# Scatter turns between the pieces of the last pair's down projection

## The chip, the cores and the metric

The kernel runs on one core of a Trainium2 chip. The metric is the device time of one execution in microseconds, as a median of several runs. The engines' short names are those of the profile: PE is TensorE (PEld its weight loads, PEldq its sequencer), DVE is VectorE, ACT is ScalarE, POOL is GpSimd, SP is SyncE, which here issues DMA transfers.

## The reference

A two-layer encoder on 256 tokens of width 2048, in float32. Each layer adds a mixer (latent attention, dilated attention and an mLSTM side by side) to `x`, and then a mixture of 16 experts, of which each token takes two:

```
for l in range(DEPTH):
    xn = rms_norm(x, norm_mix[l])
    ...
    x = x + jnp.concatenate([y_mla, y_dil, y_ml], axis=-1) @ w_out[l]
    x = x + hier_moe(rms_norm(x, norm_ffn[l]), ...)

def hier_moe(x, wg, bg, we, be, w_gate, w_up, w_down):
    ...                       # comb: weight of each expert for each token, zero but for two
    h = jax.nn.silu(jnp.einsum('bsd,edf->bsef', x, w_gate)) * jnp.einsum('bsd,edf->bsef', x, w_up)
    h = h * comb[..., None].astype(h.dtype)
    return jnp.einsum('bsef,efd->bsd', h, w_down)
```

An expert has 512 hidden units, so `w_down` is 512 by 2048 for each. The change is in the end of this part.

## The kernel before

**Experts in pairs.** The 16 experts go in eight pairs `i` = 0 to 7. For each expert up to 64 tokens (`CAP`) are gathered by a matmul with a one-hot matrix; the two experts of a pair stand side by side as 128 rows. PE then multiplies by the gate and up weights in two halves each (`expert("g0")`, `"u0"`, `"g1"`, `"u1"`), turns the product (`turn_h`), multiplies by the down weights and adds the rows back to their tokens.

**Down projection.** The down weights of an expert come in two blocks (`dn0`, `dn1`), 1024 output columns each, 16 KB a partition, laid out as four runs `k` of 1024 columns (128 hidden units each). Each block makes two tiles of 512 columns in PSUM: `dy0`, `dy1` from the first, `dy2`, `dy3` from the second, in banks 4 to 7. The two experts' matmuls use 64 columns of the array each and run side by side; a float32 matmul shows as two MATMUL records. ACT copies `dy0` and `dy2` to `Y` in SBUF (line 2509), DVE `dy1` and `dy3` (line 2191).

**Scatter.** Eight turns `sc0` to `sc7`: turn `k` multiplies columns 256k to 256k+255 of `Y` by the weighted one-hot matrix `Sw` (two matmuls, four records), and DVE adds the result to `X` (`add_moe`, line 2131). Pair `i - 1` is scattered during pair `i`. The last pair, 7, is scattered after its own down projection, in order, in banks 1, 2, 3, 0, 1, 2, 3, 0.

**The last pair** is handled apart (lines 1368 to 1383). Its weights come in halves of a block: `load_halves` (line 727) issues for each block the first half of both experts and then the second, and PE waits for the second halves in the middle of a block. A half is `k` = 0, 1 for all 1024 columns. So the loop runs `k` outside and the two tiles inside, and `dy2` and `dy3` are done together at the end:

```
for k in range(4):
    if k == 2:
        for j in range(2):
            pe.wait_ge(*loaded(f"dn{half}{j}_{i}", l))
    for q, name in enumerate(names):
        for j in range(2):
            ...
```

**Between the down projection and the last turns** stands a branch (line 1393; on DVE line 2194): if an expert had more than 64 tokens, a loop over all experts (the sweep) would compute the rest. The inputs here never take it. The two layers are written out one behind the other, so each has its own branch.

**Behind the turns.** In layer 0 DVE and ACT scale each finished pair of `X` tiles into `XN` for the next layer (`gained`; even tiles DVE, line 1522, odd tiles ACT, line 2241); PE's next matmuls, the projection `c0`, take the tiles in order, then two more projections and a matmul on the sum of squares. SP lets the next layer's loads go once `sc0` is made. In layer 1 SP sends each finished pair of `X` tiles to the output (line 774). A slot of weights may be overwritten once its last reader is done (`LAST_READER`).

All PE matmuls here are recorded by one helper, line 833; DVE's adds have line 2131.

Of the kernel before, what the change touches and what calls it, by code (L numbers as in the profile page):

```python
# [26 lines left out]
P = 128  # L27
# [172 lines left out]
def plan_banks():  # L200
# [61 lines left out]
    for i in range(NE // 2):  # L262
        b.once(f"g0_{i}", 0)
        b.once(f"u0_{i}", 1)
        b.once(f"g1_{i}", 2)
        b.once(f"ht0_{i}", 0)
        if i + 1 < NE // 2:
            for n in range(4):
                b.once(f"gx{n}_{i + 1}", 4 + n)
        b.once(f"u1_{i}", 3)  # L270
        for k in range(KT // 2):
            if k == KT // 4:
                b.once(f"ht1_{i}", 3)
            if i >= 1:
                b.once(f"sc{k}_{i - 1}", SCATTER_BANKS[k])
        b.once(f"sw_{i}", 0)
        for n in range(4):
            b.once(f"dy{n}_{i}", 4 + n)
    for k in range(KT // 2):
        b.once(f"sc{k}_{NE // 2 - 1}", LAST_BANKS[k])  # L280
    return b
# [93 lines left out]
LAST_READER.update({f"m{j}": f"{('c21', 'c12')[j % 2]}_{j // 2}" for j in range(2 * N_PAIR)})  # L375
LAST_READER.update({f"{n}{j}_{i}": f"{n}_{i}" for n in ("g0", "u0", "g1", "u1") for j in range(2) for i in range(NE // 2)})
LAST_READER.update({f"dn{half}{j}_{i}": f"dy{2 * half + 1}_{i}" for half in range(2) for j in range(2) for i in range(NE // 2)})

# [15 lines left out]
def build(nc, a, consts, onehot, lncount, out):  # L396
    with ExitStack() as ctx:
# [3 lines left out]
        def sem(name):  # L401
            return ctx.enter_context(nc.semaphore(name))
# [130 lines left out]
        dve_steps, act_steps = sem("dve_steps"), sem("act_steps")  # L533
        par_in, small_in = sem("par_in"), sem("small_in")
        pieces_in = {name: sem(f"pieces_in_{name}") for name in IN_PIECES}
        halves_in = {f"{n}{j}": sem(f"halves_in_{n}{j}") for n in ("g0", "u0", "g1", "u1", "dn0", "dn1") for j in range(2)}
        x_out, x_back = sem("x_out"), sem("x_back")
        x_in, c0_in = [sem(f"x_in{q}") for q in range(4)], [sem(f"c0_in{q}") for q in range(3)]
# [28 lines left out]
        def bank(name):  # L567
            return ps[:, BANKS.where(name), :]
# [96 lines left out]
        def _(sp):  # L665
# [14 lines left out]
            for l in range(DEPTH):  # L680
# [45 lines left out]

                def load_halves(n, w):

                    for half in range(2):
                        for j in range(2):  # L730
                            name = f"{n}{j}_{NE // 2 - 1}"
                            if half == 0:
                                sp.wait_ge(*empty(name, l))
                            part = slice(half * (SLOT // 2), (half + 1) * (SLOT // 2))
                            sp.dma_start(slot(name)[:, part], w[j][:, part]).then_inc(
                                halves_in[f"{n}{j}"] if half == 0 else slot_full[SLOTS.where(name)], 16)

                for i in range(NE // 2 - 1):
                    for half in range(2):
# [91 lines left out]
        def _(pe):  # L831
# [206 lines left out]
            for l in range(DEPTH):  # L1038
# [287 lines left out]
                for i in range(NE // 2):  # L1326
                    if i == NE // 2 - 1:
                        wait_alone(pe, *after("flags", l))
                        runs, due = sweep_due(pe)
                    if i:  # L1330
                        expert("g0", i)
                        expert("u0", i)
                    expert("g1", i)
                    turn_h(0, i)
                    if i == NE // 2 - 1:
                        written(i - 1)
                        scatter(i - 1, range(KT // 4))
                    elif i:
                        gather(i + 1)
                    expert("u1", i)  # L1340
                    if i == 0:
                        gather(1, (0,))
                        turn_h(1, 0)
                        gather(1, (1,))
                    elif i == NE // 2 - 1:
                        scatter(i - 1, (4, 5))
                        turn_h(1, i)
                        scatter(i - 1, (6, 7))
                    else:
                        written(i - 1)  # L1350
                        scatter(i - 1, range(KT // 4))
                        turn_h(1, i)
                        scatter(i - 1, range(KT // 4, KT // 2))

                    pe.wait_ge(*freed(f"sw_{i}", l))
                    pe.wait_ge(*after("gw", l, i))
                    for t in range(NT):
                        last = pe.transpose(bank(f"sw_{i}")[0:2 * CAP, t * P:(t + 1) * P], Gw[:, t, :], ident)  # L1358
                    last.then_inc(*made(f"sw_{i}"))

                    for half in range(2):
                        pe.wait_ge(*copied(f"ht{half}_{i}", l))
                    for half in range(2):
                        if half and i == 0:
                            gather(1, (2, 3))
                        w = [slot(f"dn{half}{j}_{i}").rearrange("p (k c) -> p k c", k=4) for j in range(2)]
                        for j in range(2):
                            block_in(f"dn{half}{j}_{i}")
                        if i == NE // 2 - 1:
                            names = [f"dy{2 * half + q}_{i}" for q in range(2)]  # L1370
                            for name in names:
                                pe.wait_ge(*freed(name, l))
                            for k in range(4):
                                if k == 2:
                                    for j in range(2):
                                        pe.wait_ge(*loaded(f"dn{half}{j}_{i}", l))
                                for q, name in enumerate(names):
                                    for j in range(2):
                                        own_rows = slice(j * CAP, (j + 1) * CAP)
                                        last = mm(bank(name)[own_rows, :], hs[:, k, own_rows], w[j][:, k, q * 512:(q + 1) * 512], k == 0, k == 3)  # L1380
                                    if k == 3:
                                        last.then_inc(*made(name))
                            continue
                        for q in range(2):
                            name = f"dy{2 * half + q}_{i}"
                            pe.wait_ge(*freed(name, l))
                            for k in range(4):
                                for j in range(2):
                                    own_rows = slice(j * CAP, (j + 1) * CAP)
                                    last = mm(bank(name)[own_rows, :], hs[:, k, own_rows], w[j][:, k, q * 512:(q + 1) * 512], k == 0, k == 3)  # L1390
                            last.then_inc(*made(name))

                with pe.If(due > 0):

                    i = NE // 2 - 1
                    for name in [f"sc{k}_{i - 1}" for k in range(KT // 2)] + [f"sw_{i}"] + [f"dy{n}_{i}" for n in range(4)]:
                        pe.wait_ge(*copied(name, l))
                    pe.wait_ge(sweep_dve, runs * SWEEP_DVE + 1)
                    for t in range(NT):
# [14 lines left out]
                    with pe.Fori(0, NE) as e:  # L1414
# [8 lines left out]

                        pe.wait_ge(sweep_dve, runs * SWEEP_DVE + 5 + e * 2)
                        for half in range(2):
                            w = ring[:, 4 + half, :].rearrange("p (k c) -> p k c", k=4)
                            for q in range(KT // 2):
                                o = ps[:, (4 + q // 2) if half == 0 else q // 2, q % 2 * S:(q % 2 + 1) * S]
                                for k in range(4):
                                    last = mm(o, w[:, k, q * P:(q + 1) * P], hT[:, k, :], k == 0, k == 3)  # L1430
                            last.then_inc(sweep_pe, 1)
                    wait_alone(pe, sweep_dve, runs * SWEEP_DVE + SWEEP_DVE)

                pe.wait_ge(*copied(f"sw_{NE // 2 - 1}", l))
                for n in range(4):
                    pe.wait_ge(*copied(f"dy{n}_{NE // 2 - 1}", l))
                    scatter(NE // 2 - 1, (2 * n, 2 * n + 1))


        def pcol(l, r):  # L1440
# [44 lines left out]
        def _(dve):  # L1485
# [120 lines left out]
            for l in range(DEPTH):  # L1606
# [555 lines left out]
                for i in range(NE // 2):  # L2162
# [23 lines left out]
                        add_moe(i - 1, range(KT // 4, KT // 2))  # L2186
                    dve.wait_ge(*ready(f"sw_{i}", l))
                    dve.tensor_copy(Sw, bank(f"sw_{i}")[0:2 * CAP, 0:S]).then_inc(*read(f"sw_{i}"))
                    for n in (1, 3):
                        dve.wait_ge(*ready(f"dy{n}_{i}", l))  # L2190
                        dve.tensor_copy(Y[:, n * 512:(n + 1) * 512], bank(f"dy{n}_{i}")[0:2 * CAP, :]).then_inc(*read(f"dy{n}_{i}"))  # L2191

                runs, due = sweep_due(dve)
                with dve.If(due > 0):
# [28 lines left out]
                        ins.then_inc(sweep_dve, 1)  # L2223
                    wait_alone(dve, sweep_dve, runs * SWEEP_DVE + SWEEP_DVE)
                for k in range(KT // 2):
                    add_moe(NE // 2 - 1, (k,))
                    if l + 1 < DEPTH:
                        dve.wait_ge(*copied(f"sc{k}_{NE // 2 - 1}", l))
                        gained(2 * k, l + 1)
# [309 lines left out]
def laid_out(inputs):  # L2539
# [13 lines left out]
    def columns(*rows):  # L2553
# [9 lines left out]
            "w_main": tiled(w_in[:, :, D_DQ:C_IN - 4 * H_M], CH), "w_up": up, "w_mqk": mqk,  # L2563
            "w_out_a": w["w_out"][:, :K_A * P].reshape(DEPTH, K_A, P, N_OUT, CH)[:, list(A_ROWS)].transpose(0, 3, 2, 1, 4).reshape(DEPTH, N_OUT, P, 2 * HALF_A), "w_out_b": w["w_out"][:, K_A * P:].reshape(DEPTH, K_B, P, N_BPAIR, 2, CH).transpose(0, 3, 2, 4, 1, 5).reshape(DEPTH, N_BPAIR, P, 4 * HALF_B), "w_router": tiled(router, P // GROUPS)[:, 0], "params": params, "params96": params96, "biases": biases, "x_t": x_t,
            "moe_w_gate": tiled(w["moe_w_gate"], CH), "moe_w_up": tiled(w["moe_w_up"], CH),
            "moe_w_down": tiled(w["moe_w_down"], 4 * CH)}


# [15 lines left out]
```

## Time and profile before

| | |
|---|---|
| median of 3 runs | 1823.3 us (1821.94, 1823.3, 1828.55) |
| span of the profiled execution | 1824.6 us |
| granted PE clock, mean | 0.997 |
| PE busy | 1816.0 us (100%), 12238 matmul records |
| DVE, ACT busy | 737.0 us (40%), 314.4 us (17%) |
| DMA | 546.92 MB, mean 300 GB/s |

The profiled execution is told by its span, first to last instruction; the page has no other time for it. Layer 0 ends and layer 1 begins near 917 us. A row of a timeline gives the start, the duration, the engine, the line, the operation, output and inputs, and how many alike were merged; in brackets the idle time ahead and what ended it. Matmuls overlap in their pipeline, so the time between two starts is what one costs, not its duration.

### The profile page before, as it was taken

The numbers are of one execution on the slowest core, as the hardware profiler recorded it, in microseconds if no ns is written. First come the engines' busy times: TensorE is split into PE (matmuls) and PEld (weight loads), VectorE is DVE, ScalarE is ACT, GpSimd is POOL, SyncE is SP. The second block draws the span as 40 slices with busy tenths as digits, with TensorE's granted clock in tenths as the row PEclk, the third lists the DMA queues.
The fourth block names the chain that finished last, engine by engine and source line by source line (L and its number), as shares of the span: only waits on it lengthen the run. The fifth ranks groups of instructions, "written<-read, shape, count | busy, mean of one in ns | idle before, by whom it ended". The sixth has DMA issues, their size and how long they took to land.

```text
span 1824.6 us, 28274 instructions
## 1 busy us (share of the span) xinstructions
PE 1816.0 (100%) x12238; PEld 1377.6 (76%) x12238; DVE 737.0 (40%) x1531; ACT 314.4 (17%) x846; POOL 13.9 (1%) x27
## 2 busy tenths in 40 slices
PE   9999999999999999999999999999999999999999
PEld 9788887899765667656597888878996666676665
DVE  3477665676202121121235675656761021221213
ACT  3123122212101111011021231222121011110110
POOL 1000000000000000000000000000000000000000
PEclk9999999999999999999999999999999999999999
DMA  9433343447899999999884342444579999999997
GB/s 385 165 139 142 147 168 141 189 163 287 341 425 424 426 428 426 427 427 421 346 356 150 133 178 112 167 177 153 200 283 358 421 425 427 426 428 427 426 422 305
DMA packets 51439, 546.92 MB, mean 300 GB/s; under 512 B 5872, under 2 KB 6000, under 8 KB 14576
## 3 DMA queue, kind: packets, MB, share of 16 engines
q1 hardware_dynamic: 48816, 531.47, 71.1%
q0 software_dynamic: 2496, 13.57, 2.0%
q8 instruction: 102, 1.67, 0.4%
q14 instruction: 25, 0.20, 0.0%
HBM read 540.78 MB, written 4.24 MB: 299 GB/s over the span
## 4 chain that ended last, share of the span: by engine, by line
PE 99%; DMA 0%; issue 0%; DVE 0%; SPq 0%; DVEq 0%
PE ps L833 96%; PE ps L887 1%; PE ps L1191 1%; PE ps L1299 1%; PE ps L903 0%; PE ps L895 0%; DMA ring<-in_w_lat 0%; PE ps L1358 0%; PE ps L986 0%; DVE ring L1892 0%; PE ps L1072 0%; PE ps L1099 0%; PE ps L1138 0%; DVE X L1921 0%; DVE X L2131 0%
## 5 line engine op out<-in xcount | busy, mean ns | idle before, releaser
L833 PE MATMUL ps<-ring,scr 128*64 128x256 f32 (+2 forms) x3488 | 624.6, 423 | 0.1
L833 PEld LDWEIGHTS ps<-ring,scr 128*64 128x64 f32 (+1 forms) x3488 | 336.9, 138 | 212.7 <-issue 119.3
L833 PE MATMUL ps<-ring,XN 128*128 128x256 f32 (+2 forms) x1184 | 242.2, 361 | 1.2 <-DMA ring<-in_w_lat 1.2
L833 PEld LDWEIGHTS ps<-ring,XN 128*128 128x128 f32 x1184 | 210.7, 190 | 21.7 <-issue 2.3
L833 PE MATMUL ps<-ring,X 128*128 128x256 f32 x896 | 200.6, 379 | 0.0
L833 PE MATMUL ps<-XN,ring 128*128 128x128 f32 (+1 forms) x1312 | 195.8, 306 | 0.0
L833 PEld LDWEIGHTS ps<-XN,ring 128*128 128x128 f32 x1312 | 180.2, 191 | 12.7 <-issue 3.1
L833 PEld LDWEIGHTS ps<-ring,X 128*128 128x128 f32 x896 | 169.6, 190 | 22.7
L833 PE MATMUL ps<-PR,scr 128*64 128x256 f32 (+2 forms) x704 | 173.8, 402 | 0.0
L2167 DVE TENSOR_TENSOR v_mla<-scr,ps 128x256 f32<-128x256 f32 x32 | 13.5, 421 | 390.6 <-PE ps L833 390.6
L833 PE MATMUL ps<-BIAS,scr 128*64 128x256 f32 (+1 forms) x608 | 157.2, 414 | 0.0
L833 PE MATMUL ps<-XN,scr 128*64 128x256 f32 (+1 forms) x480 | 141.3, 451 | 0.0
L833 PEld LDWEIGHTS ps<-v_mla,PR 128*128 128x128 f32 x1024 | 117.3, 193 | 4.2 <-issue 4.2
L833 PE MATMUL ps<-v_mla,PR 128*128 128x128 f32 x1024 | 120.2, 277 | 0.0
L833 PE MATMUL ps<-PR,prob 128*128 128x256 f32 x512 | 117.7, 382 | 2.3 <-issue 2.3
L833 PEld LDWEIGHTS ps<-PR,scr 128*64 128x64 f32 (+1 forms) x704 | 98.0, 144 | 25.6 <-issue 3.4
L833 PEld LDWEIGHTS ps<-PR,prob 128*128 128x128 f32 x512 | 94.6, 190 | 21.3 <-issue 9.8
L2191 DVE COPY prob<-ps 128x512 f32<-128x512 f32 x32 | 22.1, 692 | 207.4 <-PE ps L833 207.4
L833 PEld LDWEIGHTS ps<-BIAS,scr 128*64 128x64 f32 x608 | 81.8, 137 | 29.5 <-issue 2.9
L2494 ACT ACTIVATE scr<-ps,par 128x128 f32<-128x128 f32 x240 | 64.7, 407 | 220.1 <-PE ps L833 220.1
L2131 DVE TENSOR_TENSOR X<-X,ps 128x512 f32<-128x512 f32 x128 | 87.9, 688 | 28.0 <-PE ps L833 27.1
L833 PEld LDWEIGHTS ps<-XN,scr 128*64 128x64 f32 x480 | 65.3, 137 | 34.2 <-issue 25.0
(276 smaller groups left out, 1454.7 us busy)
## 6 DMA issues: line engine op xcount, KB each, us to landing
ring<-in_moe_w_gate SPq DMA_DIRECT2D x38, 2048.0 KB, 20.2
ring<-in_w_main SPq DMA_DIRECT2D x36, 2048.0 KB, 9.5
ring<-in_moe_w_down SPq DMA_DIRECT2D x32, 2048.0 KB, 22.2
ring<-in_moe_w_up SPq DMA_DIRECT2D x30, 2048.0 KB, 17.3
ring<-in_w_out_a SPq DMA_DIRECT2D x16, 1280.0 KB, 6.0
PR<-in_moe_w_up SPq DMA_DIRECT2D x10, 2048.0 KB, 16.3
XN<-in_moe_w_down SPq DMA_DIRECT2D x10, 2048.0 KB, 19.2
ring<-in_moe_w_up SPq DMA_DIRECT2D x20, 1024.0 KB, 21.5
```

The lines of the kernel that those rows point to most:

```text
L833: return pe.matmul(o, lhsT, rhs, start=start, stop=stop, skip_group_check=True)
L887: last = pe.transpose(bank(name)[:, (kt * NT + t) * P:(kt * NT + t + 1) * P], prob[:, u % 2, j, t, kt * P:(kt + 1) * P], ident)
L1191: last = pe.transpose(bank(f"xt{j}")[:, q * P:(q + 1) * P], X[:, 4 * g + q, t * P:(t + 1) * P], ident)
L1299: last = pe.transpose(bank(name)[:, q * 2 * CAP:(q + 1) * 2 * CAP], gated[:, (2 * half + q) * P:(2 * half + q + 1) * P], ident)
L2131: dve.tensor_tensor(x, x, bank(name), ALU.add).then_inc(*read(name))
L2167: dve.tensor_tensor(gated[:, half * CH:(half + 1) * CH], sgs[:, half * CH:(half + 1) * CH], bank(f"u{half}_{i}")[0:2 * CAP, 0:CH], ALU.mul ...
L2191: dve.tensor_copy(Y[:, n * 512:(n + 1) * 512], bank(f"dy{n}_{i}")[0:2 * CAP, :]).then_inc(*read(f"dy{n}_{i}"))
L2494: ins = act.activation(XG[:, 4 * n + k, :], bank(name)[:, k * 2 * CAP:(k + 1) * 2 * CAP], ACT.Copy, scale=pcol(l, R_FFN + 4 * n + k))
```

## The change

The down weights are laid out anew, in all eight pairs: a block is four runs `n` of 256 output columns, and each holds its four `k`. A matmul of 512 columns reads two runs of 256, which lie 1024 elements apart. The last pair now finishes a piece of columns before it begins the next: `dy0`, `dy1`, `dy2` with 512 columns, and `dy3`, `dy4` with 256 each (`dy4` in bank 4, which `dy0` had). Its second block is loaded in three pieces for each expert (a half and two quarters). The turns 0 and 1 stand between `dy1` and `dy2`, 2 and 3 between `dy2` and `dy3`, 4 and 5 between `dy3` and `dy4`, and 6 and 7 stay behind the branch. DVE's adds follow, so that in layer 0 the `gained` steps of the first six turns come behind DVE's branch, without the adds. The sweep reads its weights in the new layout and waits for more banks. Lines that follow from this alone are left out:

```diff
+    b.once(f"dy4_{NE // 2 - 1}", 4)
...
+LAST_READER.update({f"dn1{j}_{NE // 2 - 1}": f"dy4_{NE // 2 - 1}" for j in range(2)})
...
-                    for half in range(2):
+                    for lo, hi in ((0, 2), (2, 4)) if n != "dn1" else ((0, 2), (2, 3), (3, 4)):
...
+                    def down(name, half, lo, hi):
+
+                        w = [slot(f"dn{half}{j}_{i}").rearrange("p (n k c) -> p n k c", n=4, k=4) for j in range(2)]
+                        pe.wait_ge(*freed(name, l))
+                        for k in range(4):
+                            for j in range(2):
+                                own_rows = slice(j * CAP, (j + 1) * CAP)
+                                last = mm(bank(name)[own_rows, 0:(hi - lo) * CH], hs[:, k, own_rows], w[j][:, lo:hi, k, :], k == 0, k == 3)
+                        last.then_inc(*made(name))
...
+                    if i == NE // 2 - 1:
+                        for j in range(2):
+                            block_in(f"dn0{j}_{i}")
+                        down(f"dy0_{i}", 0, 0, 2)
+                        last_blocks(0)
+                        down(f"dy1_{i}", 0, 2, 4)
+                        pe.wait_ge(*copied(f"sw_{i}", l))
+                        pe.wait_ge(*copied(f"dy0_{i}", l))
+                        scatter(i, (0, 1))
+                        for j in range(2):
+                            block_in(f"dn1{j}_{i}")
+                        down(f"dy2_{i}", 1, 0, 2)
+                        pe.wait_ge(*copied(f"dy1_{i}", l))
+                        scatter(i, (2, 3))
+                        for j in range(2):
+                            pe.wait_ge(third_in[j], 16 * (l + 1))
+                        down(f"dy3_{i}", 1, 2, 3)
+                        pe.wait_ge(*copied(f"dy2_{i}", l))
+                        scatter(i, (4, 5))
+                        last_blocks(1)
+                        down(f"dy4_{i}", 1, 3, 4)
+                        break
...
-                pe.wait_ge(*copied(f"sw_{NE // 2 - 1}", l))
-                for n in range(4):
+                for n in (3, 4):
                     pe.wait_ge(*copied(f"dy{n}_{NE // 2 - 1}", l))
-                    scatter(NE // 2 - 1, (2 * n, 2 * n + 1))
+                    scatter(NE // 2 - 1, (n + 3,))
...
+                    last = i == NE // 2 - 1
+                    for n, lo, w in ((1, 512, 512), (3, 1536, CH), (4, 1536 + CH, CH)) if last else ((1, 512, 512), (3, 1536, 512)):
                         dve.wait_ge(*ready(f"dy{n}_{i}", l))
...
+                        if last and n != 4:
+                            add_moe(i, {1: (0, 1, 2, 3), 3: (4, 5)}[n])
...
                 for k in range(KT // 2):
-                    add_moe(NE // 2 - 1, (k,))
+                    if k >= 6:
+                        add_moe(NE // 2 - 1, (k,))
                     if l + 1 < DEPTH:
...
-            "moe_w_down": tiled(w["moe_w_down"], 4 * CH)}
+            "moe_w_down": tiled(w["moe_w_down"], CH).reshape(DEPTH, NE, 2, 4, P, 4 * CH).swapaxes(3, 4).reshape(DEPTH, NE, 2, P, SLOT)}
```

## Rows read from the trace of the kernel before

**Rows 1.** The page's head and its first part.
```profile
span 1824.6 us, 28274 instructions
...
PE 1816.0 (100%) x12238; PEld 1377.6 (76%) x12238; DVE 737.0 (40%) x1531; ACT 314.4 (17%) x846; POOL 13.9 (1%) x27
```

**Rows 2.** Waits of PE, whole span: us in total, times, longest.
```profile
PE ps L833 <- issue: 2.3, 2, 1.8
PE ps L833 <- DMA ring<-in_w_lat: 1.2, 1, 1.2
PE ps L833 <- DVE eps L1494: 1.1, 1, 1.1
PE ps L833 <- DVE ring L1892: 0.3, 2, 0.2
```

**Rows 3.** PE timeline, layer 0's end: start us, us, what, [idle before].
```profile
893.00 0.64 PE L833 MATMUL ps<-ring,scr 128*64 128x512 f32 x1
...
899.92 7.32 PE L833 MATMUL ps<-ring,scr 128*64 128x512 f32 x32
...
909.05 2.40 PE L833 MATMUL ps<-PR,prob 128*128 128x256 f32 x10 [1.82 <-issue]
...
911.96 5.02 PE L833 MATMUL ps<-PR,prob 128*128 128x256 f32 x22 [0.51 <-issue]
...
916.82 18.36 PE L833 MATMUL ps<-ring,XN 128*128 128x192 f32 x114
```

**Rows 4.** PE timeline, layer 1's end.
```profile
1800.27 0.64 PE L833 MATMUL ps<-ring,scr 128*64 128x512 f32 x1
...
1807.18 7.16 PE L833 MATMUL ps<-ring,scr 128*64 128x512 f32 x32
...
1814.28 7.17 PE L833 MATMUL ps<-PR,prob 128*128 128x256 f32 x32
```

**Rows 5.** PE timeline, two changes of tile shape in the last pair.
```profile
1787.73 1.46 PE L833 MATMUL ps<-PR,prob 128*128 128x256 f32 x6
...
1789.12 0.43 PE L833 MATMUL ps<-BIAS,scr 128*64 128x256 f32 x1
...
1789.38 0.38 PE L833 MATMUL ps<-BIAS,scr 128*64 128x256 f32 x1
...
1795.86 0.38 PE L833 MATMUL ps<-BIAS,scr 128*64 128x256 f32 x1
...
1796.17 1.99 PE L833 MATMUL ps<-PR,prob 128*128 128x256 f32 x8
...
1798.01 0.38 PE L1299 MATMUL ps<-K,v_mla 128*128 128x128 f32 x2
```

**Rows 6.** Lines 1393 (branch) and 1376 (wait): ns min/median/max, first and last start.
```profile
L1393 PEldq COMPARE_BRANCH  x2: 3308/4204/5100, 903.8 to 1810.8; - x2
...
L1376 PEldq EVENT_SEMAPHORE  x4: 51/51/51, 893.7 to 1810.6; - x4
```

**Rows 7.** DVE timeline, layer 1's end.
```profile
1800.76 0.42 DVE L2188 COPY PR<-ps 128x256 f32<-128x256 f32 x1
...
1814.38 0.69 DVE L2191 COPY prob<-ps 128x512 f32<-128x512 f32 x1 [6.29 <-PE ps L833]
...
1815.87 1.99 DVE L2131 TENSOR_TENSOR X<-X,ps 128x512 f32<-128x512 f32 x3 [0.80 <-PE ps L833]
...
1821.49 0.69 DVE L2131 TENSOR_TENSOR X<-X,ps 128x512 f32<-128x512 f32 x1 [0.18 <-PE ps L833]
```

**Rows 8.** DVE and PE timelines, where the next layer begins.
```profile
918.34 0.35 DVE L1522 TENSOR_SCALAR XN<-X,par 128x256 f32<-128x256 f32 x1
...
926.01 0.43 DVE L1620 TENSOR_TENSOR scr<-PR 128x256 f32<-128x256 f32 x1
...
937.19 0.59 PE L833 MATMUL ps<-scr,ones 128*128 128x256 f32 x2
```

**Rows 9.** SP's DMA issues, second down block of layer 1.
```profile
1775.60 11.12 SPq L735 DMA_DIRECT2D ring<-in_moe_w_down  x4
```

More of the change, by code:

```diff
@@ L535, in build @@
         pieces_in = {name: sem(f"pieces_in_{name}") for name in IN_PIECES}
+        third_in = [sem(f"third_in{j}") for j in range(2)]
         halves_in = {f"{n}{j}": sem(f"halves_in_{n}{j}") for n in ("g0", "u0", "g1", "u1", "dn0", "dn1") for j in range(2)}
@@ L727, in load_halves @@
                 def load_halves(n, w):
-                    for half in range(2):
+                    for lo, hi in ((0, 2), (2, 4)) if n != "dn1" else ((0, 2), (2, 3), (3, 4)):
                         for j in range(2):
                             name = f"{n}{j}_{NE // 2 - 1}"
-                            if half == 0:
+                            if lo == 0:
                                 sp.wait_ge(*empty(name, l))
-                            part = slice(half * (SLOT // 2), (half + 1) * (SLOT // 2))
+                            part = slice(lo * (SLOT // 4), hi * (SLOT // 4))
                             sp.dma_start(slot(name)[:, part], w[j][:, part]).then_inc(
-                                halves_in[f"{n}{j}"] if half == 0 else slot_full[SLOTS.where(name)], 16)
+                                halves_in[f"{n}{j}"] if lo == 0 else slot_full[SLOTS.where(name)] if hi == 4 else third_in[j], 16)
                 for i in range(NE // 2 - 1):
@@ L1362, in _, with last_blocks @@
                         pe.wait_ge(*copied(f"ht{half}_{i}", l))
+                    def down(name, half, lo, hi):
[6 more added lines that the diff above has]
+                        last.then_inc(*made(name))
+                    def last_blocks(half):
+                        for j in range(2):
+                            pe.wait_ge(*loaded(f"dn{half}{j}_{i}", l))
+                    if i == NE // 2 - 1:
[12 more added lines that the diff above has]
+                        scatter(i, (2, 3))
+                        for j in range(2):
+                            pe.wait_ge(third_in[j], 16 * (l + 1))
[5 more added lines that the diff above has]
+                        break
                     for half in range(2):
@@ L1365, in _ @@
                             gather(1, (2, 3))
-                        w = [slot(f"dn{half}{j}_{i}").rearrange("p (k c) -> p k c", k=4) for j in range(2)]
                         for j in range(2):
                             block_in(f"dn{half}{j}_{i}")
[L1369 to L1383, printed above, removed]
-                        for q in range(2):
[L1385 to L1391, printed above, removed]
+                        for q in range(2):
+                            down(f"dy{2 * half + q}_{i}", half, 2 * q, 2 * q + 2)
                 with pe.If(due > 0):
                     i = NE // 2 - 1
-                    for name in [f"sc{k}_{i - 1}" for k in range(KT // 2)] + [f"sw_{i}"] + [f"dy{n}_{i}" for n in range(4)]:
+                    for name in [f"sc{k}_{i - 1}" for k in range(KT // 2)] + [f"sw_{i}"] + [f"dy{n}_{i}" for n in range(5)] + [f"sc{k}_{i}" for k in range(6)]:
                         pe.wait_ge(*copied(name, l))
@@ L1425, in _ @@
                         for half in range(2):
-                            w = ring[:, 4 + half, :].rearrange("p (k c) -> p k c", k=4)
+                            w = ring[:, 4 + half, :].rearrange("p (n k c) -> p n k c", n=4, k=4)
                             for q in range(KT // 2):
@@ L1429, in _ @@
                                 for k in range(4):
-                                    last = mm(o, w[:, k, q * P:(q + 1) * P], hT[:, k, :], k == 0, k == 3)
+                                    last = mm(o, w[:, q // 2, k, q % 2 * P:(q % 2 + 1) * P], hT[:, k, :], k == 0, k == 3)
                             last.then_inc(sweep_pe, 1)
                     wait_alone(pe, sweep_dve, runs * SWEEP_DVE + SWEEP_DVE)
-                pe.wait_ge(*copied(f"sw_{NE // 2 - 1}", l))
-                for n in range(4):
+                for n in (3, 4):
                     pe.wait_ge(*copied(f"dy{n}_{NE // 2 - 1}", l))
-                    scatter(NE // 2 - 1, (2 * n, 2 * n + 1))
+                    scatter(NE // 2 - 1, (n + 3,))
         def pcol(l, r):
@@ L2188, in _ @@
                     dve.tensor_copy(Sw, bank(f"sw_{i}")[0:2 * CAP, 0:S]).then_inc(*read(f"sw_{i}"))
-                    for n in (1, 3):
+                    last = i == NE // 2 - 1
+                    for n, lo, w in ((1, 512, 512), (3, 1536, CH), (4, 1536 + CH, CH)) if last else ((1, 512, 512), (3, 1536, 512)):
                         dve.wait_ge(*ready(f"dy{n}_{i}", l))
-                        dve.tensor_copy(Y[:, n * 512:(n + 1) * 512], bank(f"dy{n}_{i}")[0:2 * CAP, :]).then_inc(*read(f"dy{n}_{i}"))
+                        dve.tensor_copy(Y[:, lo:lo + w], bank(f"dy{n}_{i}")[0:2 * CAP, 0:w]).then_inc(*read(f"dy{n}_{i}"))
+                        if last and n != 4:
+                            add_moe(i, {1: (0, 1, 2, 3), 3: (4, 5)}[n])
                 runs, due = sweep_due(dve)
```

## The prediction

> **What bounds the kernel now.** I read the page's head, then what TensorE (PE) waits for, then its timeline at the end of each of the two layers, where the change lies. The head shows PE busy for 1816.0 of 1824.6 us [rows 1]. All that its matmuls wait for is a few us; the largest is 2.3 us in two waits that no data releases ("issue") [rows 2]. So the kernel is a queue of matmuls, and an edit pays only if it takes matmul time or an idle stretch of PE away. Near the change there is one such stretch. In layer 0 the second half of the down projection starts at 899.92 and the first scatter matmul at 909.05, 9.13 us later; eight turns then take until 916.82, with a 0.51 us hole [rows 3]. In layer 1 the same second half needs 1814.28 - 1807.18 = 7.10 us, with no hole behind it [rows 4]. Layer 0 thus loses 9.13 - 7.10 = 2.03 us ahead of the turns, and within them 7.77 us less 6.91 and 0.1 for the change of shape: some 0.75. The 6.91 are 32 matmuls a step of 0.216 us apart (layer 1's 32 take 7.17; less the last one's own 0.38 and that 0.1, over 31 steps). Together 2.8 us, all that can be won there; layer 1 has nothing to win.
>
> **Matmul work.** Per layer the last pair's down projection stays 13.8 us (1800.27 to 1814.1) [rows 4] and the turns 6.9 us. The eight matmuls with 512 columns that made half of the old second block become sixteen with 256 (32 more weight loads and matmuls in the stream). Two 256-column steps take 2 x 0.216 us [rows 5], one of 512 takes 6.91/16 = 0.43 [rows 4]: nothing added.
>
> **Two runs in the moving operand.** In all eight pairs the weights now lie by blocks of 256 columns, so a 512-column matmul reads two runs of 256. No row of before has that. Lower bound: 0. Upper bound from the nearest rows: each run charged like a matmul of its own, 2 x 0.216 - 0.43, some 0.003 us, for 496 such steps (248 per layer: 7 pairs x 32, and 24): 1.4 us. I take 0, since the steps of one run show no cost per run.
>
> **Switching between the two kinds of matmul.** Down steps use 64-column tiles in pairs, scatter turns full 128-column tiles. Into full tiles: 1795.86 to 1796.17 is 0.31 instead of 0.216, and eight matmuls from 1796.17 end at 1798.01 instead of 1797.90; 0.20 together. Back: 1787.73 plus six steps is 1789.03, the next starts at 1789.12, and the one after 0.26 later instead of 0.216; 0.13 together [rows 5]. Before there was one switch, down to scatter. Now there are three round trips more per layer: 3 x 0.33 = 1.0 us each, 2.0 us in all. Lower bound 0, if the queue covers them; I take 2.0, since each switch shown paid.
>
> **The branch.** Behind the down projection stands a branch over a loop that is skipped. PE's sequencer takes 5.10 us over it in layer 0 (from 903.8, so until 908.9; the scatter starts at 909.05) and 3.31 us in layer 1 (from 1810.8, until 1814.1; scatter at 1814.28) [rows 3, 4, 6]. This is the stall of layer 0, and layer 1 just escapes: the sequencer stood 3.3 us ahead of the array. It stood there because the wait ahead of the last 32 instructions was passed at 1810.6, as the array began them (1807.18 + 3.44), the branch was reached 0.2 us later, and those instructions last 3.4 us [rows 4, 6]. After the change the last 32 instructions, dy4's, are 256 wide and last 8 x 0.216 = 1.73, with the switch 1.86. The same distances give a lead of 1.86 - 0.2 = 1.66 us and a stall of 3.31 - 1.66 = 1.6 us in each layer. Bounds: 0 (the half before passed its wait at 893.7, 2.8 us before the array came to it [rows 3, 6]; such a lead covers all), and 5.10 - 1.66 = 3.4. I take 1.6, from the wait that stands where the new one will stand. The hole of 0.75 inside layer 0's turns came right behind the branch and has no data releaser; I let it go with the stretch of code that is moved.
> The page Runtime: NRT & Kernel Launch of the Trainium skill, section Instruction fetch mechanics, says that instructions are prefetched in sequence alone and that a taken branch to a target outside the window stalls until the page is fetched. By it both layers would stall, whatever the lead; the trace agrees in layer 0 (2.03 us) and not in layer 1 (none). The sum by it would lie between the forecast's and the +6.0 of the second rival. TensorE: Matmul & The Clock Gate (its table) gives PE a queue of 64. By it the sequencer would be 64 instructions ahead, which now reaches back over dy4 (32) and the turns before it, and the branch would be hidden; the wait at 1810.6, with no lead, does not agree. The sum by it would be the first rival's.
>
> **Waits of the new order.** Turn pairs (0,1), (2,3), (4,5) each wait for a copy of the block before last: dy0's copy has dy1's 3.4 us, dy1's has turns 0 and 1 and dy2, dy2's has turns 2 and 3 and dy3 (1.9 + 1.7) against 0.69 us for a copy [rows 7]. Behind each stands all of PE, so an uncovered copy would cost up to 0.8 us. dy3's copy has turns 4 and 5 and dy4. Only dy4's is close: VectorE starts such a copy 0.1 us after PE's next matmul (1814.38 against 1814.28 [rows 4, 7]), a 256-wide one takes 0.42, and turn 6 covers it with 0.87 us; without that cover 0.2. In VectorE's queue the adds of turns 0 to 5 now stand between the copies; two adds of 0.69 fit into each 1.7 us of down work.
>
> **Behind the last turn** nothing changes in layer 1: the last add starts at 1821.49 and the span ends 3.1 us later [rows 1, 7]; the earlier output transfers only leave sooner. In layer 0 VectorE and ScalarE also scale X into XN. VectorE now does six such steps (0.35 each) in a row behind its own branch, then adds 6 and 7. From the start of dy4's copy: 1.5 us to the first step (1814.38 to 1815.87 [rows 7]), 2.2 for six, 2.0 for the rest, so 5.7. The next layer's first projection starts at 1.6 + 1.9 - 0.1 = 3.4 by the same clock and asks for a pair of XN tiles every 1.29 us (0.161 us a matmul, eight a pair [rows 3]): first at 3.4 (there at 1.9), last at 12.4. The sum of squares, ready at 926.4, is used at 937.19 [rows 8]. All hidden; were there no branch stall, the first tile would be 0.4 us late.
>
> **DMA.** The second block comes in six transfers, not four. The old four were issued from 1775.60 to 1786.7 [rows 9], for a block used at 1807.18 [rows 4]: 20 us of cover, so two more issues cost nothing (at most their own 0.9 us with the cover gone). The next layer's loads, let go by turn 0, leave some 7 us sooner, the third of them (it waits for dy4) 2 us later; PE had no DMA wait there to lose or gain [rows 2].
>
> **Sum** on the profiled execution (1824.6 us; the page has its span and no time around it): layer 0: 2.0/2 + 1.6 - 2.8 = -0.2; layer 1: 1.0 + 1.6 = +2.6. Together +2.4, 1827.0. The median of the three runs is 1823.3, 1.3 below the span, which gives 1825.7.
>
> **Rivals.**
> *The branch is hidden* (sequencer far enough ahead). Layer 0: 1.0 + 0.4 - 2.8 = -1.4; layer 1: 1.0 + 0.2. Sum -0.2: 1823.1; with the switches covered too, -2.2: 1821.1. For it: the lead of 2.8 at 893.7. Against it: the wait at 1810.6.
> *The branch takes 5.1 us in both layers.* 1.0 + 3.4 - 2.8 and 1.0 + 3.4: +6.0, 1829.3; in layer 0 alone +4.2, 1827.5. For it: code moves, and one of two branches took that long. Against: the other did not.
> *Slower outright: the second run of a 512-column operand costs a restart.* A first step behind a switch is 0.04 to 0.05 longer [rows 5]; with that on each of 496 steps, 23 us: 1849. It decides the sign from (9.1 - 2.4)/496 = 0.014 us a step. Against: nothing in rows of one run hints at it.
> Faster by over 0.5% has no mechanism: PE's waits come to 4.9 us in all, the start of the kernel among them [rows 2].
>
> **How the numbers follow.** Forecast 0.60, long branch in one layer or both 0.15, branch hidden 0.20, restart per run 0.04, something else faster 0.01. A measurement of this kernel can tell about 0.5%, 9.1 us, from no change; all but the last two lie within. The range reaches from the hidden branch with covered switches, 1821, to the long branch with 1.4 us for the two runs, 1830.7, and I let the spread of the runs (1821.94 to 1828.55) take the low end to 1820.5. Faster 0.01, same 0.95, slower 0.04.
>
> **What will show it.** The branch rows: each over 3 us, and a PE hole of 1 to 2 us ahead of turn 6 in both layers, none of 0.75 behind it in layer 0. Starts 0.3 us apart at each of the six switches. Steps of 512 columns still 0.43 apart in pairs 0 to 6. No PE wait for a copy or a DMA between dy0 and dy4. The forecast is wrong if layer 1's end grows by less than 1 us or more than 4, or if the time changes outside the two layer ends.

## The result and the profile after

The changed kernel took 1830.71 us (median of 5 runs, 1829.05 to 1835.14), the kernel before 1822.99 beside it: a ratio of 1.0031, 95% interval 1.002 to 1.0043; the two medians alone lie 7.7 us apart, 1.0042, at the upper end of that interval. On a second occasion it was 1.0022 (1.0011 to 1.0032). So by the ratios it is slower by 0.2 to 0.3%, 4 to 6 us, within the 0.5% that counted as no change; the forecast was +2.4 us. The profiled span went from 1824.6 to 1829.1 us.

The page's head, TensorE's waits over the whole span, and its branch, in the changed kernel (answering [rows 1, 2, 6]; line 836 is the matmul helper, line 1411 the branch):

```profile
span 1829.1 us, 28344 instructions
...
PE 1817.1 (99%) x12270; PEld 1378.0 (75%) x12270; DVE 737.2 (40%) x1533; ACT 313.8 (17%) x846; POOL 13.8 (1%) x27
...
PE ps L836 <- issue: 4.3, 2, 2.2
PE ps L836 <- DMA ring<-in_w_lat: 2.7, 1, 2.7
...
L1411 PEldq COMPARE_BRANCH  x2: 3882/3910/3938, 912.3 to 1819.9; - x2
```

PE's timeline at the end of layer 0, after (answering [rows 3]): the five pieces of down work, the turns two by two between them, and the next layer's first matmul.

```profile
894.01 0.64 PE L836 MATMUL ps<-ring,scr 128*64 128x512 f32 x1
...
901.03 1.99 PE L836 MATMUL ps<-PR,prob 128*128 128x256 f32 x8
902.95 3.65 PE L836 MATMUL ps<-ring,scr 128*64 128x512 f32 x16
906.54 1.99 PE L836 MATMUL ps<-PR,prob 128*128 128x256 f32 x8
908.46 1.95 PE L836 MATMUL ps<-ring,scr 128*64 128x256 f32 x16
910.34 1.99 PE L836 MATMUL ps<-PR,prob 128*128 128x256 f32 x8
912.26 1.95 PE L836 MATMUL ps<-ring,scr 128*64 128x256 f32 x16
916.34 1.96 PE L836 MATMUL ps<-PR,prob 128*128 128x256 f32 x8 [2.13 <-issue]
918.14 17.11 PE L836 MATMUL ps<-ring,XN 128*128 128x192 f32 x106
```

The same at the end of layer 1 (answering [rows 4]), and VectorE's last add there [rows 7]:

```profile
1801.60 0.64 PE L836 MATMUL ps<-ring,scr 128*64 128x512 f32 x1
...
1817.92 1.99 PE L836 MATMUL ps<-PR,prob 128*128 128x256 f32 x8
1819.85 1.95 PE L836 MATMUL ps<-ring,scr 128*64 128x256 f32 x16
1823.98 1.96 PE L836 MATMUL ps<-PR,prob 128*128 128x256 f32 x8 [2.18 <-issue]
...
1825.98 0.69 DVE L2148 TENSOR_TENSOR X<-X,ps 128x512 f32<-128x512 f32 x1 [0.18 <-PE ps L836]
```

Where the 4.5 us of span came from, stretch by stretch: up to dy0 of layer 0 it is 894.01 against 893.00, +1.0 (below). Layer 0's end, dy0 to the next layer's first matmul: 24.13 against 23.82, +0.3. The whole middle, 918.14 to 1801.60: 883.46 against 883.45, nothing. Layer 1's end, dy0 to the last add: 24.38 against 21.22, +3.2. In both layers the time is in one hole ahead of turn 6, and the six switches.

The +1.0 was not forecast. The first weights are waited for 2.7 us instead of 1.2, and the first projection starts 0.8 us later; and right behind that wait the granted clock is 0.5 (the 1.2 GHz level, half of the other) for 3.4 us, so that this projection takes 1.6 us longer. Against that, a stretch at the low level near 455 us, which every profile here has, lasts 3.4 us where it lasted 6.8 before, some 1.7 us less lost. That makes 0.7; 0.3 us is left open. The first two rows are the first projection before and after. The third is a row by stretch: its bounds and length, the busy time of PE, PEld, DVE, ACT and POOL, the granted clock, and the DMA's share and rate.

```profile
6.95 20.61 PE L833 MATMUL ps<-ring,XN 128*128 128x192 f32 x128 [1.22 <-DMA ring<-in_w_lat]
7.72 22.21 PE L836 MATMUL ps<-ring,XN 128*128 128x192 f32 x128 [2.69 <-DMA ring<-in_w_lat]
...
7.60:10.90 3.30, 3.18 (x10) 3.21 (x11) 0.62 (x2) 0.97 (x3) 0.00 (x0) 0.50 1.03 409
```

The table gives these two ends for all kernels run (start to start, from the timelines), and PE's branch. The expectations below count layer 1 only to its last matmul, 0.4 to 0.7 us sooner than the last add.

| kernel | layer 0 end, us | layer 1 end, us | branch, us (layer 0, 1) | ratio (95%) |
|---|---|---|---|---|
| before | 23.82 | 21.22 | 5.10, 3.31 | |
| before_again | 24.89 | 21.46 | 4.72, 3.57 | 1.0003 (0.9992 to 1.0014) |
| after | 24.13 | 24.38 | 3.88, 3.94 | 1.0031 (1.002 to 1.0043) |
| after_again | 23.68 | 25.46 | 3.44, 3.93 | 1.0022 (1.0011 to 1.0032) |
| before_no_branch | 20.90 | 21.10 | none | 0.9991 (0.9979 to 1.0002) |
| after_no_branch | 22.92 | 22.40 | none | 1.0002 (0.9992 to 1.0012) |
| after_short_skip | 23.01 | 22.39 | 0.25, 0.36 | 1.0006 (0.9996 to 1.0016) |
| layout_only | 22.98 | 21.88 | 3.84, 3.56 | 0.9997 (0.9986 to 1.0007) |
| turns_behind | 25.43 | 23.81 | 5.01, 3.48 | 1.0025 (1.0016 to 1.0034) |
| two_pieces | 26.12 | 22.17 | 6.27, 3.80 | 1.0017 (1.0008 to 1.0026) |
| after_else | 28.08 | 22.40 | 7.19, 3.61 (the jump) | 1.0029 (1.0018 to 1.0041) |
| before_else | 25.81 | 21.16 | 5.78, 4.35 (the jump) | 1.0039 (1.0025 to 1.0054) |

### The profile page after: what moved, and what is told of

It reads as the page before. It is cut to its first block, busy times and chain, and to the rows that moved or that the text cites. A ratio compares the mean times of both kernels' runs of the same rounds, so it can differ in the third digit from the quotient of the medians.

```text
span 1829.1 us, 28344 instructions
## 1 busy us (share of the span) xinstructions
PE 1817.1 (99%) x12270; PEld 1378.0 (75%) x12270; DVE 737.2 (40%) x1533; ACT 313.8 (17%) x846; POOL 13.8 (1%) x27
## 4 chain that ended last, share of the span: by engine, by line
PE 99%; DMA 0%; issue 0%; DVE 0%; SPq 0%; DVEq 0%
PE ps L836 96%; PE ps L890 1%; PE ps L1194 1%; PE ps L1302 1%; PE ps L906 0%; DMA ring<-in_w_lat 0%; PE ps L898 0%; PE ps L1361 0%; PE ps L989 0%; DVE ring L1909 0%; PE ps L1102 0%; PE ps L1075 0%; PE ps L1141 0%; DVE X L1938 0%; DVE X L2148 0%
## 5 line engine op out<-in xcount | busy, mean ns | idle before, releaser
L2209 DVE COPY prob<-ps 128x512 f32<-128x512 f32 (+1 forms) x34 | 22.4, 660 | 199.4 <-PE ps L836 199.4
```

The costliest lines, as they stand in the source:

```text
L2209: dve.tensor_copy(Y[:, lo:lo + w], bank(f"dy{n}_{i}")[0:2 * CAP, 0:w]).then_inc(*read(f"dy{n}_{i}"))
```

## The experiments

**The kernel before, once more** (no edit).

> The kernel before, unchanged, profiled a second time. Theory A (the 2.8 us that layer 0 loses at its branch belong to the way the code lies): the hole is there again, second down half to first scatter matmul 9.1 us in layer 0 and 7.1 in layer 1, branch rows 5.1 and 3.3 us, span within 1 us of 1824.6. Theory B (they are an accident of the one profiled execution, which would explain why the medians differ by 7.7 us and the two profiled spans by 4.5): layer 0 shows 7.1 to 7.5 us as layer 1 does, both branches near 3.3 us, span 1820.5 to 1822.5. Time: ratio 1.000 by both.

Theory A held: the hole at layer 0's branch came again, with a second hole behind it. In its PE timeline the branch (4.72 us) leaves 1.44 and 1.06 us; a third hole is new, PE waiting 0.96 us for the second half of the second down block. In layer 1 a branch of 3.57 us, longer than the 3.31 of the first profile, leaves a hole of 0.16.

```profile
903.76 3.65 PE L833 MATMUL ps<-ring,scr 128*64 128x512 f32 x16 [0.96 <-DMA ring<-in_moe_w_down]
908.86 2.40 PE L833 MATMUL ps<-PR,prob 128*128 128x256 f32 x10 [1.44 <-issue]
912.32 5.01 PE L833 MATMUL ps<-PR,prob 128*128 128x256 f32 x22 [1.06 <-issue]
```

**The branch taken out of the changed kernel, and of the kernel before.**

```diff
-                with pe.If(due > 0):
+                if False:
```

> The changed kernel without the sweep loop and its branch on PE (the part that computes tokens beyond 64 of an expert is left out). Theory A (the hole of 2.1 us ahead of turn 6 in each layer is the branch): both holes go, dy4 to turn 6 is 0.3 us; the layer ends shorten by 2 x 2.1, less up to 0.4 each for the copy of dy4, now uncovered: 3.4 to 4.3 us off the span, some 1825. Ratio to before 1.001. Rival C (PE waits there for VectorE's copies of dy3 and dy4): the holes stay and so does the span, 1829. Ratio 1.003.

> The kernel before without the sweep loop and its branch on PE (the part that computes tokens beyond 64 of an expert is left out). Theory A: layer 0's loss of 2.8 us goes, layer 1 stays: span 1821.8 if the profiled execution of before is typical. Theory B: nothing to gain beyond what the repeated profile of before shows. In both, the changed kernel without branch stays behind this one by its six switches more per layer, 2 x 1.0 us, and up to 0.8 for the copies of dy4: 2.0 to 2.8 us. Ratio 0.9985 (A) or 1.000 (B).

Theory A held in both for the layer ends. In the changed kernel without the branch, dy4 is followed by turn 6 without a hole in either layer (1817.23 plus eight steps of 0.216 is 1818.96; the turn starts 0.15 later, the switch), so no copy was waited for, and rival C is out. What PE now waits for in layer 0 is VectorE's first XN tile.

```profile
1817.23 1.95 PE L836 MATMUL ps<-ring,scr 128*64 128x256 f32 x16
1819.11 1.99 PE L836 MATMUL ps<-PR,prob 128*128 128x256 f32 x8
...
916.46 8.85 PE L836 MATMUL ps<-ring,XN 128*128 128x192 f32 x53 [0.79 <-DVE XN L1539]
```

Without branches the changed kernel stays 2.0 us behind in layer 0 (0.8 of it that wait) and 1.3 in layer 1: the switches, some 1.2 to 1.3 us a layer. In time it is 1.0002 against 0.9991, some 2 us. The profiled span of the kernel before without the branch, 1824.0, is above A's 1821.8: 1.4 us of that lies between the layer ends, where the granted clock is 0.5 from 1358.9 to 1365.8, 6.8 us instead of the 3.4 before.

**The new layout alone.** The last pair's loop, q outside, two halves, no turn in between:

```diff
+                            if q and i == NE // 2 - 1:
+                                for j in range(2):
+                                    pe.wait_ge(*loaded(f"dn{half}{j}_{i}", l))
...
-last = mm(bank(name)[own_rows, :], hs[:, k, own_rows], w[j][:, k, q * 512:(q + 1) * 512], k == 0, k == 3)
+last = mm(bank(name)[own_rows, :], hs[:, k, own_rows], w[j][:, 2 * q:2 * q + 2, k, :], k == 0, k == 3)
```

> The new layout of the down weights alone: the last pair finishes dy0, dy1, dy2, dy3 one after the other, its blocks in two halves, no scatter turn in between. Theory A (a second run in the operand is free, a branch ahead of which 32 instructions of 512 columns lie is nearly hidden): steps of 512 columns 0.43 us apart in all pairs, layer ends as before (layer 1: 7.1 us from dy2's start to the first turn), span within 1 us of the kernel before. Rival D (the two runs cost, spread over all pairs): 0.003 us a step gives +1.4 us, 0.01 gives +5, and the changed kernel's loss is found here. Ratio 1.000 (A), 1.001 to 1.003 (D).

0.9997, and a span of 1822.7: no cost of the two runs shows, and rival D is out; its smallest cost, +1.4 us, lies just above the interval's upper end (1.0007, +1.3 us), and the middle of the changed kernel, with 224 such steps, was 0.01 us from that of before (0.15 between the second profiles). Layer 1's end is 0.4 to 0.7 us longer than in the two profiles of before, with holes of 0.37 and 0.15 us.

**The changed kernel once more** (no edit).

> The changed kernel, unchanged, profiled a second time. From the start of the last pair's down projection to the next layer's first matmul it took 24.1 us in layer 0, and to its last matmul 24.0 in layer 1; before it was 23.8 and 24.9 (layer 0, two profiles), 20.8 and 21.0 (layer 1). Theory A (the loss is the two layer ends): 24 and 24 again, the wait for the first transfer at the kernel's start, 2.7 us in the first profile, back at 1.0 to 1.6; ratio 1.0015 to 1.002 with before on the same chip. Rival E (something more, at the start or between the layer ends): the 2.7 us come again, or other stretches than the ends are longer by 1 us or more than in both profiles of before; ratio 1.003.

Theory A held for the start: the wait for the first transfer was 1.4 us, so the 2.7 of the first profile is not the changed kernel's own; over all twelve profiles this wait is 1.0 to 2.7. Layer 0's hole followed its branch (3.44 us, hole 1.68; first profile 3.88 and 2.13). Layer 1's end was 1.1 us longer than in the first profile, all of it inside the last two turns, whose eight matmuls took 3.05 instead of 1.96 us. No hole did that: behind the hole of 2.18 us the granted clock, 1.00 for the first three of these matmuls, was 0.50 for the rest (from 1821.04 on), and each then cost twice the time. In the first profile the same hole was followed by a clock of 1.00.

```profile
913.53 1.97 PE L836 MATMUL ps<-PR,prob 128*128 128x256 f32 x8 [1.68 <-issue]
...
1820.31 3.05 PE L836 MATMUL ps<-PR,prob 128*128 128x256 f32 x8 [2.18 <-issue]
...
1820.20:1821.00 0.80, 0.69 (x3) 0.67 (x4) 0.00 (x0) 0.00 (x0) 0.00 (x0) 1.00 0.09 26
1821.10:1823.20 2.10, 2.10 (x6) 1.27 (x4) 0.69 (x1) 0.00 (x0) 0.00 (x0) 0.50 0.00 0
```

**All turns behind the branch** (DVE's adds go with them).

```diff
-                        scatter(i, (0, 1))
...
-                        scatter(i, (2, 3))
...
-                        scatter(i, (4, 5))
...
+                scatter(NE // 2 - 1, range(6))
                 for n in (3, 4):
```

> The changed kernel with all eight scatter turns behind the branch, so that the down pieces follow one another and six switches less per layer are paid. Theory A: the branch is reached when 32 instructions are left, here still those of dy4 (1.73 us), so the hole of 2.1 us ahead of the first turn stays in both layers and only the switches go, 1.0 us per layer: layer ends near 23.1 and 22.9 us. Rival F (what precedes dy4 decides how far the sequencer is ahead, and without waits for copies it gets further ahead): holes under 1 us, layer ends near 21.5. Ratio 1.001 (A) or 1.000 (F).

Holes stayed, so rival F is out, but they were not 2.1 each: 2.76 us in layer 0 (branch 5.01), 1.48 in layer 1 (branch 3.48) with 0.90 behind it. The ends (25.43 and 23.81) did not shrink by the switches as A had it. In layer 0 the longer branch took 0.6 us of that back and the granted clock 1.7: it was 0.50 from 912.38 to 915.79, right behind the hole, and the 32 matmuls took 8.86 us instead of 7.17 [rows 4]. In layer 1 it was the second hole, at a clock of 1.00.

```profile
911.92 8.86 PE L836 MATMUL ps<-PR,prob 128*128 128x256 f32 x32 [2.76 <-issue]
...
912.40:915.70 3.30, 3.30 (x9) 2.58 (x9) 1.42 (x3) 0.51 (x1) 0.00 (x0) 0.50 0.39 83
...
1820.01 1.99 PE L836 MATMUL ps<-PR,prob 128*128 128x256 f32 x8 [1.48 <-issue]
1822.91 5.34 PE L836 MATMUL ps<-PR,prob 128*128 128x256 f32 x24 [0.90 <-issue]
```

**Without the third piece** (loads and adds follow).

```diff
-                        down(f"dy3_{i}", 1, 2, 3)
-                        pe.wait_ge(*copied(f"dy2_{i}", l))
-                        scatter(i, (4, 5))
                         last_blocks(1)
-                        down(f"dy4_{i}", 1, 3, 4)
+                        down(f"dy3_{i}", 1, 2, 4)
```

> The changed kernel without its third piece: the second block in two halves, dy3 with 512 columns, turns 0 to 3 between the pieces and 4 to 7 behind the branch. The last 32 instructions ahead of the branch now last 16 x 0.43 / 2 = 3.4 us. Theory A: a branch of 3.3 to 3.9 us leaves a hole of 0 to 0.5 us, two round trips of switches cost 0.7 us per layer: layer ends near 21.6 us each (layer 0 more if its branch takes 5). Rival F: the holes are those of the changed kernel, 2.1 us, and the ends near 23.5. Ratio 1.000 (A) or 1.0015 (F).

Layer 1 as A had it: branch 3.80, hole 0.34. Layer 0 not: its branch took 6.27 us and left 2.80. The difference, 6.27 - 3.80 = 2.47, is the difference of the holes, 2.46: what the array has queued ahead of the branch is the same 3.5 us in both. In layer 0 the granted clock is again 0.50 behind the hole, from 915.02 to 918.43, and the 16 matmuls take 5.38 us where layer 1's take 3.69.

```profile
L1404 PEldq COMPARE_BRANCH  x2: 3797/5031/6265, 907.8 to 1816.4; - x2
...
914.28 5.38 PE L834 MATMUL ps<-PR,prob 128*128 128x256 f32 x16 [2.80 <-issue]
...
915.10:918.40 3.30, 3.30 (x10) 2.59 (x9) 2.05 (x4) 0.83 (x2) 0.00 (x0) 0.50 1.00 418
...
1820.38 3.69 PE L834 MATMUL ps<-PR,prob 128*128 128x256 f32 x16 [0.34 <-issue]
```

**A short skip.** In the sweep, on PE alone:

```diff
-                    for e in range(NE):
+                    for e in range(1):
...
-                                for k in range(KT):
+                                for k in range(1):
...
-                                for k in range(4):
+                                for k in range(1):
```

> The changed kernel with the skipped sweep cut down to some 150 instructions on PE instead of over 1000 (its loops over k and over the 16 broadcast rows run once; this leaves out most of the part that computes tokens beyond 64 of an expert, which does not run here). Theory A, with the branch's time being the fetch of code that lies far ahead: the branch rows fall below 1 us and the holes ahead of turn 6 go, layer ends near 22.9 and 21.7 us, as without the branch. Rival G (a taken branch costs PE 3.3 us or more whatever it jumps over): branch rows 3.3 to 3.9 us, holes 2.1 us, ends 24 us. Ratio 1.000 (A) or 1.002 (G).

Theory A held in full: the same branch, over 29 matmuls in the code instead of 242, takes 0.25 and 0.36 us, and both holes are gone.

```profile
L1411 PEldq COMPARE_BRANCH  x2: 247/304/361, 910.1 to 1815.5; - x2
...
1815.51 1.95 PE L836 MATMUL ps<-ring,scr 128*64 128x256 f32 x16
1817.39 1.99 PE L836 MATMUL ps<-PR,prob 128*128 128x256 f32 x8
```

**The branch turned round**, in both kernels: the usual path first, the jump behind it.

```diff
-                with pe.If(due > 0):
+                with pe.If(due < 1):
+                    last_turns()
+                with pe.Else():
                     ...
+                    last_turns()
```

> The changed kernel with the branch turned round: the usual path runs straight into turns 6 and 7, and the jump over the sweep (complete, as in the changed kernel) stands behind them. Theory A (the branch costs its own 3.4 to 5 us, less what the array still has queued when the sequencer reaches it, 32 instructions): no hole ahead of turn 6, dy4 to turn 6 is 0.31 us. In layer 1 the jump lies behind the last matmul, under the last add and the output transfer: end near 21.7 us, 2.3 to 3 less than in the changed kernel. In layer 0 the last 32 instructions are turns 6 and 7 and half of dy4, 2.9 us, so that the next layer's first matmul is 0.5 to 2 us late, of which 0.8 would be lost to VectorE's XN anyway: 22.7 to 24. Ratio to before 1.0005. Rival H (the hole belongs to the short pieces and their waits, not to the jump): layer 1 stays at 24, ratio 1.002.

> The kernel before with the branch turned round in the same way. Theory A: in layer 1 the jump is out of the way, end 20.7 us instead of 20.8 and 21.0; in layer 0 32 instructions of the turns, 3.5 us, stand ahead of the jump, so that a jump of 3.4 us costs 0 to 0.3 and one of 5 us 1.7: 21 to 22.6 us instead of 23.8 and 24.9. That would be 1.5 to 4 us less than before, ratio 0.998 to 0.999. Rival I (layer 0's jump is a long one wherever it stands, or the next layer's start suffers): layer 0 stays near 24, ratio 1.000.

The holes ahead of the turns went, so H is out and the cost is the jump's. In layer 1 of the changed kernel A came true: the jump (1827.26 to 1830.87) ran under the output, which ended 3.2 us after the last add as before. But layer 0's jump only moved, and grew: the next projection waited 5.96 us in the one kernel and 4.76 in the other, behind jumps of 7.19 and 5.78 us. I had expected 32 queued instructions ahead of the jump, 2.9 and 3.5 us of turns. In `before_else` the jump's row begins at 912.18 and the last turn matmul at 912.99, a lead of 0.8 us with four matmul records left; in `after_else` it is 914.68 and 915.69, 1.0 us with five. Why the sequencer had so little lead there stays open. Behind these two holes the granted clock was 0.50 until 924.03 and 926.07, which cost the projection some 3 and 2 us more (half of the time from its start).

In layer 1 of `before_else` the span ended 5.6 us after the last add (1824.70 to 1830.3) instead of 3.1. The jump was over at 1826.35; the span waited for the output's transfers, which took 2.1 to 4.1 us to land. No run shows why they were slower. So `before_else`, whose two ends are only 1.9 us over those of before, is some 7 us slower: 3 more lie in the clock and 2.5 behind the last add. Rival I, with 24 us and a ratio of 1.000, was nearer than A for layer 0 and too low as well.

The first fence is the next layer's first matmul in `after_else`. The second is that of `before_else`, with VectorE's last add of layer 1, the branch rows, the clock behind the hole, and the output transfers' time to landing before and in `before_else`.

```profile
922.03 8.24 PE L836 MATMUL ps<-ring,XN 128*128 128x192 f32 x37 [5.96 <-issue]
```

```profile
906.20 7.17 PE L833 MATMUL ps<-PR,prob 128*128 128x256 f32 x32
918.12 12.08 PE L833 MATMUL ps<-ring,XN 128*128 128x192 f32 x55 [4.76 <-issue]
...
L1400 PEldq COMPARE_BRANCH  x4: 82/2220/5784, 902.6 to 1822.0; - x4
...
1824.70 0.69 DVE L2136 TENSOR_TENSOR X<-X,ps 128x512 f32<-128x512 f32 x1 [0.17 <-PE ps L833]
...
918.10:924.00 5.90, 5.88 (x18) 5.90 (x19) 4.61 (x5) 3.56 (x4) 0.00 (x0) 0.50 1.02 367
...
DMA to landing us min/median/max: 2.0/2.1/2.1
DMA to landing us min/median/max: 2.1/2.8/4.1
```

No version run beats the kernel before beyond its interval with the sweep complete.

## Why the prediction was right, and where its sizes were off

- *The result as a whole.* No change was forecast, and slower by 2.4 us within it; that came true, but the 4.0 to 5.7 us of the ratios are about twice that, and the median of 1830.71 stands at the range's upper end, 1830.7.
- *The branch.* The stall came in both layers, as forecast; its size was too small, because the branch's duration was mis-sized. The branch was reached at 912.3 and 1819.9, as the array began dy4 (912.26, 1819.85): a lead of 1.7 us, forecast 1.66. I took 3.31 us, the shorter of the two rows of before, for its length; it took 3.88 and 3.94. Hence holes of 2.13 and 2.18 us where 1.6 stood in the sum: 1.1 us too little over both layers. Taking the branch out, or its target near, removes the holes; that is shown. The reason given for the lead is not: the wait ahead of the last 32 instructions, passed as the array begins them. After, the last wait row ahead of dy4 (line 1370) stands at 1816.5, 3.3 us before the array began dy4. In `turns_behind` the wait for dy4's weights (line 1379) was passed at 905.9, 1.3 us before dy4's first matmul (907.26), and the branch was reached with 18 matmul records left, not fewer. The lead came out right by luck in that sense; what holds the sequencer there stays open. The first row is of the changed kernel, the second of `turns_behind`.

```profile
L1370 PEldq EVENT_SEMAPHORE  x38: 51/51/1867, 499.3 to 1816.5; - x38
L1379 PEldq EVENT_SEMAPHORE  x2: 51/51/51, 905.9 to 1816.2; - x2
```

- *The switches.* Right: 1.0 us a layer forecast, 1.2 to 1.3 between the two kernels without branch.
- *Layer 0's second hole of 0.75.* It went in both profiles of the changed kernel, as assumed. But a second hole, of 0.90 us, came up in layer 1 with all turns behind the branch, so letting it go for good was a guess, and what makes it stays open.
- *Two runs in the operand.* Right: the middle of the kernel kept its length to 0.01 us (0.15 in the second profiles), and the layout alone measured 0.9997.
- *Copies and VectorE.* Right: no copy was waited for. The first XN tile, forecast 0.4 us late without a stall, was 0.79 and 0.89 late.
- *DMA.* Right for the changed kernel; the 20 us of cover were read from layer 1 alone. In layer 0 the second profile of before shows PE waiting 0.96 us for that block.
- *The sum.* The layer ends moved by +0.3 and +3.2 us (first profiles), forecast -0.2 and +2.6. The ends' 3.5 are thus the forecast's 2.4 and the branch's 1.1. The measured 4.0 and 5.7 us (1.0022, 1.0031) are 0.5 and 2.2 more than the ends' 3.5; the interval of the second timing (2.0 to 5.8 us) holds them. Of its 4.0 us, 2.9 to 3.6 go without the branch or with a short skip (1.0006 and 1.0002 in place of 1.0022).
- *The granted clock.* The prediction has no term for it. It fell behind the new hole in layer 1 in the second profile (1.1 us) and behind the first wait in the first (1.6 us). In the second timing its mean over the runs was 0.9978 after and 0.9985 before; 0.0007 of 1825 us is 1.3 us, an estimate of what it added there. With it, layer 1's end grew by 4.0 to 4.2 us in the second profile, at the bound of 4 beyond which the prediction called itself wrong; without it, by about 3. Outside the ends the time changed at the kernel's start, up to layer 0's dy0, by +1.0 us in the first profiles and -0.6 in the second.

The page Runtime: NRT & Kernel Launch of the Trainium skill, section Instruction fetch mechanics, has a taken branch stall when its target lies outside what was fetched in sequence. The runs agree: 3.3 to 7.2 us over 242 matmuls' code, 0.25 to 0.36 us over 29; the fetch itself is in no row. The prediction read layer 1 before as disagreeing, but its branch row of 3.31 us is the same stall, hidden by what the array still had queued. How much of it PE feels is its length less that.

## What to carry to other kernels

On an engine that is busy all the time, a new order can win only the holes that its timeline shows, and every change of tile shape that it adds is paid. Before work is moved ahead of a branch that skips much code, look at the branch's own row and at how long the instructions just ahead of it last: narrow ones hide less of it. A hole of the array can cost more than its length: look at the granted clock of the stretch behind it before a longer row is put down to another hole. Profile the kernel before twice when the holes in question are a few us: some of them come and go.

## What the runs showed of the hardware

PE's sequencer took 3.3 to 7.2 us over the same skipped loop, another length in each kernel and layer: 3.88 in layer 0 of the changed kernel, 6.27 in layer 0 of the variant without the third piece. It repeated within 0.5 us for the same kernel (5.10 and 4.72; 3.31 and 3.57; 3.88 and 3.44; 3.94 and 3.93). The conditional branch was reached as the array began the last 16 matmul records, whether these take 1.7 us (branch at 1819.9, their start at 1819.85) or 3.4 (1816.4 and 1816.39), and in layer 0 of `turns_behind` with 18 left; the jump behind the turns with 4 and 5 left in layer 0 (0.8 and 1.0 us), and 11 and 5 in layer 1. A branch that is not taken took 0.08 us (the 82 in `before_else`).

The granted clock went from 1.0 to 0.5 (2.4 to 1.2 GHz) behind several idle stretches of PE: behind the wait for the first weights in three profiles (`turns_behind`, 2.3 us; `after_else`, 2.4; `after`, 2.7), behind layer 0's holes of 2.76, 2.80, 4.76 and 5.96 us, and behind one of the two holes of 2.18 us in layer 1 (`after_again`, not `after`). The matmuls behind it then cost 1.1 to some 3 us more.
